# Attention softmax maxima: one reduction over the first map's first two PSUM banks in place of one per bank

## What is computed

```python
def diff_attention(q, k, v, lam):
    ...
    def one_block(qblk):
        s = jnp.einsum('bqhmd,bkhmd->bhmqk', qblk, k,
                       preferred_element_type=jnp.float32) * ATTN_SCALE
        p = jax.nn.softmax(s, axis=-1)
        a = p[:, :, 0] - lam * p[:, :, 1]
        return jnp.einsum('bhqk,bkhv->bqhv', a.astype(v.dtype), v)
```

## Time and profile before

| what | value |
| --- | --- |
| median of 3 runs | 2750.31 us (2748.93 to 2750.7) |
| span of the profiled execution | 2745.3 us |
| median less that span | 5.0 us |
| PE busy in the span | 2680.3 us |
| DVE busy in the span | 1638.9 us |
| ACT busy in the span | 1020.4 us |

### The profile page before, as it was taken

How to read it: one execution, slowest core, us unless ns; L and a number is a source line. 1 busy time by engine, 2 the same in 40 slices (tenths; PEclk the granted TensorE clock), 3 DMA queues, 4 the chain that set the end, 5 groups by cost and what they waited for, 6 DMA issues and landing times.

```text
span 2745.3 us, 39843 instructions
## 1 busy us (share of the span) xinstructions
PE 2680.3 (98%) x16386; PEld 2203.7 (80%) x16386; DVE 1638.9 (60%) x1815; ACT 1020.4 (37%) x1394; POOL 1010.2 (37%) x612
## 2 busy tenths in 40 slices
PE   8999998999999999999999999999999999999997
PEld 5888778888788888788888888888777888888885
DVE  6496129876944456555546666666869433444436
ACT  5332127763433343444452222222334222222222
POOL 0253115104588864222221111111144754445552
PEclk9999999999999999999999999999999999999998
DMA  7211530022321233111121111111032112121112
GB/s 239 70 31 39 184 123 1 2 78 85 114 62 51 58 108 92 48 45 46 49 58 44 40 40 40 40 39 38 27 92 62 54 39 62 47 62 54 54 31 100
DMA packets 260432, 174.79 MB, mean 64 GB/s; under 512 B 5792, under 2 KB 252960, under 8 KB 259104
## 3 DMA queue, kind: packets, MB, share of 16 engines
q1 hardware_dynamic: 258816, 169.69, 20.5%
q10 hardware_dynamic: 1440, 2.59, 0.3%
HBM read 163.87 MB, written 8.39 MB: 63 GB/s over the span
## 4 chain that ended last, share of the span: by engine, by line
PE 68%; issue 13%; DVE 9%; POOL 4%; ACT 2%; DVEq 2%; SPq 1%; DMA 0%; POOLq 0%; ACTq 0%
PE PS L2637 10%; PE PS L2638 10%; PE PS L2639 10%; PE PS L2209 10%; PE PS L2211 9%; PE PS L2210 9%; POOL Wlo L616 3%; DVE qR L1695 2%; ACT exp L1055 1%; DVE acol L1747 1%; PE PS L2741 1%; PE PS L2748 1%; PE PS L2316 1%; PE PS L2548 1%; PE PS L2826 1%
## 5 line engine op out<-in xcount | busy, mean ns | idle before, releaser
L616 POOL TENSOR_TENSOR Wlo<-Wraw,Whi 128x1024 fp32r<-128x1024 f32 (+1 forms) x140 | 339.4, 2424 | 1018.8 <-ACT Whi L831 1002.4
L2209 PE MATMUL PS<-Bh,Whi 128*128 128x512 f32 x1184 | 472.5, 399 | 6.2 <-DVE Bl L1486 2.8
L2211 PE MATMUL PS<-Bh,Wlo 128*128 128x512 f32 x1184 | 461.8, 390 | 0.0
L2210 PE MATMUL PS<-Bl,Whi 128*128 128x512 f32 x1184 | 461.2, 389 | 0.0
L2209 PE MATMUL PS<-Hh,Whi 128*128 128x512 f32 x672 | 267.2, 398 | 6.8 <-issue 1.7
L2209 PEld LDWEIGHTS PS<-Bh,Whi 128*128 128x128 f32 x1184 | 222.1, 188 | 58.9 <-DVE Bl L1486 6.9
L2211 PE MATMUL PS<-Hh,Wlo 128*128 128x512 f32 x672 | 261.9, 390 | 0.0
L2211 PEld LDWEIGHTS PS<-Bh,Wlo 128*128 128x128 f32 x1184 | 222.2, 188 | 47.5
L2210 PEld LDWEIGHTS PS<-Bl,Whi 128*128 128x128 f32 x1184 | 222.5, 188 | 44.5 <-issue 0.7
L2210 PE MATMUL PS<-Hl,Whi 128*128 128x512 f32 x608 | 236.9, 390 | 0.0
L831 ACT ACTIVATE Whi<-Wraw 128x1024 fp32r<-128x1024 f32 (+1 forms) x140 | 144.4, 1032 | 127.7 <-PE PS L2211 126.5
(11 more groups left out here) (465 smaller groups left out, 5929.1 us busy)
## 6 DMA issues: line engine op xcount, KB each, us to landing
Wraw<-in_w_in SPq DMA_DIRECT2D x64, 512.0 KB, 4.0
adaV<-in_ada_w SPq DMA_DIRECT2D x16, 1024.0 KB, 5.3
Wraw<-in_odd_w_in SPq DMA_DIRECT2D x32, 512.0 KB, 4.9
Wraw<-in_w_up SPq DMA_DIRECT2D x32, 512.0 KB, 4.1
Wraw<-in_w_down SPq DMA_DIRECT2D x28, 512.0 KB, 4.3
Wraw<-in_even_w_in SPq DMA_DIRECT2D x24, 512.0 KB, 3.7
adaW<-in_ada_w SPq DMA_DIRECT2D x8, 1024.0 KB, 11.4
Wraw<-in_even_w_out SPq DMA_DIRECT2D x14, 512.0 KB, 3.8
```

The costliest lines, as they stand in the source:

```text
L616: pool.tensor_tensor(Wlo[:, slot, 0:tiles, :], Wraw[:, slot, 0:tiles, :], Whi[:, slot, 0:tiles, :].bitcast(F32), ALU.subtract).then_inc(lo ...
L2209: mm(out, Whi[:, u % 2, k, :], hi[:, k, c], start=(k == 0), stop=False)
L2210: mm(out, Whi[:, u % 2, k, :], lo[:, k, c], start=False, stop=False)
L2211: return mm(out, Wlo[:, u % 2, k, :], hi[:, k, c], start=False, stop=(k == KT - 1))
```

## The change

The first map's first two banks (1024 columns, contiguous in PSUM) are reduced by one instruction, which waits until the second of them is written. The last 256 columns are reduced as before, and the maximum of partial maxima is over two columns in place of three.

```diff
-            for i in range(3):
-                dve.wait_ge(sem("s0_psum"), 3 * b + i + 1)
-                dve.reduce_max(acol[:, s, i:i + 1], bank(i, 512 if i < 2 else 256), AX.X)
+            for i in range(2):
+                dve.wait_ge(sem("s0_psum"), 3 * b + i + 2)
+                dve.reduce_max(acol[:, s, i:i + 1], PS[:, S0:S0 + 1024] if i == 0 else PS[:, S0 + 1024:S0 + NK], AX.X)
             dve.drain()
-            dve.tensor_reduce(acol[:, s, 5:6], acol[:, s, 0:3], AX.X, ALU.max, negate=True).then_inc(sem("negmax"), 1)
+            dve.tensor_reduce(acol[:, s, 5:6], acol[:, s, 0:2], AX.X, ALU.max, negate=True).then_inc(sem("negmax"), 1)
```

## The result

The changed kernel takes 2766.46 us (median) against 2750.18 us before: ratio 1.006, 95% interval 1.005 to 1.0071, so 13.8 to 19.5 us slower. Five of its six runs lie between 2766.20 and 2766.66 us; the sixth, in the slow state, took 7112.06 us, for which no reason is known, and is left out of the ratio but not of the median (2766.36 without it). The profiled execution took 2766.27 us, 1.8 more than its span of 2764.5.

A forecast was written before the change was run, and what follows sets the result against it. Bound taken: the attention stage's serial loop of waits. Per-block +0.58 for the later start less 0.06 saved, summed with smaller late-block terms to +14.4 us, plus 5.0 around the span: 2764.7 us, range 2760.5 to 2768.9.

The forecast's parts named there:

- The loop in series: Attention stage: score matmuls, DVE maxima and both exps wait in turn, 5.92 us a block; added time lengthens the block.
- The moved wait: First reduction waits for the second S0 bank, not the first: starts 0.58 us later, bounds 0.43 and 0.73.
- The saved work: DVE maxima: one 1024-column reduction for two of 512 columns saves 0.06 us per block, at most 0.15.
- Late blocks: Blocks where GpSimd's L692 holds up L1763 and DVE starts late: +0.33 us each instead of +0.52.
- Blocks 1 to 7: Early attention blocks: block 1 covered by PE work, blocks 2 and 3 +0.52 us each, later ones +0.515, +0.43 or +0.33.
- W: Loss from the first reduction waiting for the second bank, 0.52 us in each ordinary attention block.
- L1763 delays no block: Sign of being right: the one-column DVE instruction L1763 no longer makes any attention block start late.
- a granted clock under 1: Sign of being wrong: TensorE's granted clock falls below full.
- G: Follow-up theory's extra loss in blocks 3 to 6, from DVE meeting GpSimd's key splits.
- The clock rival: Attention stage: more PE idling drops TensorE from 2.4 to 1.2 GHz, 128 us more, 2892 us; chance 0.02.
- The sum: All attention blocks together: +14.4 us, span 2745.3 to 2759.7, plus 5.0 us around it: 2764.7 us.
- DVE's instruction count: Rival: fewer DVE instructions decide, saving 0.06 to 0.15 us in all 32 blocks, 2748.3 to 2745.5 us; chance 0.04.

The follow-up runs named there:

- The wait alone: Kernel before with its three reductions kept, the first also waiting for the second bank's event; 2768.93 us, ratio 1.0069.
- the gated kernel: Changed kernel with GpSimd's key splits 1 to 3 and other large splits of blocks 8 to 16 held for the previous block's combination; 2763.73 us, ratio 1.0052.
- the other pairing: Kernel before with bank 0 reduced alone, then bank 1 and the last 256 columns in one instruction; 2759.59 us, ratio 1.0035.

## Why the prediction was right

**The loop in series**: right. 0.33 us of extra DVE work cost 0.33 us an ordinary block, with DVE about 90% busy before and PE at 98% of the program.

**The moved wait**: right, start 1.68 to 1.70 us behind the first score matmul where 1.70 was forecast from the modelled matmul end and block 1's lag of 0.04. Neither bound of the delay, 0.43 or 0.73, occurred.

**The saved work**: right, 0.06. The wait alone has period 6.51, the change 6.44 (0.07 apart). The 1024-column read took 1.224 us for the forecast 1.215.

**Late blocks**: right from block 8 on. L1763 took 0.30 to 0.32 us there, no block started late and all periods but one are 6.43 to 6.46. The 24 blocks were forecast at 20 x 0.515 + 4 x 0.33 = 11.6 and came to 12.08; 0.34 of the difference is one block whose L1749 started late (below).

**Blocks 1 to 7**: here a step failed. The term was 2 x 0.52 + 2 x 0.52 + 0.43 + 0.33 = 2.8 us; measured 8.35, of which W alone is 2.9 (the gated kernel). I said that the combination would end 0.5 later and that this slack stays, and let "released at the same time" stand for all of GpSimd's work. That was read at L692, one instruction in every other block. While blocks 2 to 5 are computed GpSimd runs the key splits nearly end to end (409.05 to 424.86, then from 427.77), and there a combination that comes 0.36 us later (L1763 at 414.18 in place of 413.82, and 0.55 later against GpSimd) finds it already running. Of the signs that the prediction names, "L1763 delays no block" didn't hold, and "a granted clock under 1", a sign of being wrong, was there.

By the changed kernel's periods block 4 lost 1.1 us and block 5 1.6 beyond W, with DVE's maxima 1.7 and 2.2 us late; block 3 lost 1.5 and block 6 1.2 beyond it, with the clock at half in the scores of block 3, and in the transposes and value products ahead of the scores of block 6. So 2.7 of the 5.4 us beyond W are G with the clock at full, and 2.7 go with the clock. Block 3's part is not the change's own, since the old form paid 1.2 to 1.4 there in three of four profiles.

The Trainium skill (SBUF — State Buffer, "Who interferes with whom") has VectorE and GpSimd share a port pair that one instruction holds to its end; the traces agree, the ends being within 0.04 us of each other, and the gates took the stall away. That L1763's lateness is what GpSimd's order makes of it is shown; that it is this port is the page's reading.

**The clock rival**: given 0.02 for the whole stage at 1.2 GHz, and that did not occur. A small form of it did, two stretches of 3.4 us, about 2.7 us together. The first follows a stretch in which PE was idle for half of 5.3 us. I had argued from a row with the granted clock at 1.00 over 20 us, and the same blocks in other executions of the old form have the clock at half, so one profile couldn't settle it. Idle time alone doesn't decide it either: 2.72 and 2.84 us busy of 5.30 came without a fall (the kernel before, and the gated change) and 2.52 with one. The second is seen only where the change, or the wait alone, stands in the early blocks without the gates (three profiles). There it comes behind a PE stall of 1.7 to 1.8 us for L1744, which L1763 had held up.

**The sum**: the shift of the span was 19.2 us where 14.4 was forecast, and above the high bound of 18.6. The median came out 1.8 above my number and not 4.8 because a second term was off the other way. I took 5.0 us around the span from the median, but it is 1.8 to 1.9. The profiled execution before was one of the shorter ones (2745.3 + 1.9 = 2747.2 against a median of 2750.2); the second profile of it has 1.6 us more in the early stretch and 2.0 more behind block 31. With 1.9 in place of 5.0 the forecast would have been 2761.6 and its range 2757.4 to 2765.8, and the measured 2766.46 lies outside. That the time fell into the range is in part luck; the mechanism and its 0.52 us a block are not.

**DVE's instruction count**: fell, as argued. The saving is real (0.07 us a block) and is outweighed eight to one. The rule of the Trainium skill (VectorE: DVE Perf Modes, "The TRN2 errata") that the prediction names is stated for operations that read SBUF. These reductions read PSUM, and the runs show a saving for them as well.

Open: what makes the clock fall in one execution of the same kernel and not in the next, and whether G brings on the second fall. Neither was tried. What is said of the early blocks rests on one profiled execution of each kernel.

## What to carry to other kernels

Merging reductions over banks that are still being filled gives up an overlap: here 0.58 of the 0.60 us by which the first one had been ahead of the second came back on the path. In a loop in series, look at when each input's event comes and how long the reader is already running by then; the saving counts only once all inputs are there. Before trusting slack that is "unchanged", list what the other engines run in the same interval in each part of the stage, the first blocks too, and take more than one execution's profile before taking what lies around the span from a median.

## What the hardware showed beside

A DVE instruction over one column with operands in SBUF waited up to 2.85 us for a GpSimd one over 1280 columns, and the order turned over on a shift of 0.55 us between the two. In the changed kernel one block (24) has 0.42 us of idle time before L1749, 0.35 more than in the others, for which the profile shows no releaser. The same gap stands in block 24 of the other pairing and of the gated change:

```profile
558.46 1.56 DVE L1747 TENSOR_REDUCE acol<-PS 128x1 f32<-128x1024 f32 x2 [0.49 <-PE PS L2551]
560.44 0.15 DVE L1749 TENSOR_REDUCE acol<-acol 128x1 f32<-128x2 f32 x1 [0.42 <-issue]
```

The two kernels with the change in some blocks alone have one of 0.40 us ahead of their one-column instruction, at 549.58 and 595.84. The kernel before has 0.30 us of idle time in block 22 ahead of L1761 (533.82), which its profile puts down to ACT's exp and which cost nothing. A fixed place in DVE's stream would fit; that wasn't tested, and what it is stays open.
